# A sparse expert stage on one Trainium2 core: even down products right behind the pair's sum, and expert 0's rows turned inside the second gather

## The chip, the core and the metric

The kernel runs on one core of a Trainium2 chip. The metric is the device time in microseconds of one execution. In the profile PE is TensorE, DVE VectorE, ACT ScalarE, POOL GpSimd and SP the sync engine, whose queue (SPq) issues nearly all loads.

## What is computed

Two layers of a diffusion transformer on 256 tokens of width 1024 in float32: layer 0 has differential attention over tokens and context, layer 1 a pooling mixer, and behind each stands a mixture of 32 experts of which every token uses two. The reference, cut to the expert part:

```python
def moe(h_flat, router_w, router_b, w_gate, w_up, w_down):
    experts, gates = route(h_flat, router_w, router_b)      # 2 of 32 for each of 256 tokens
    ...                                                     # rows sorted by expert
    def expert_block(args):
        xb, e = args
        return (jax.nn.silu(xb @ w_gate[e]) * (xb @ w_up[e])) @ w_down[e]
    ys = lax.map(expert_block, (xs, block_e)).reshape(n_slots, d)
    ys = ys * slot_gate[:, None].astype(ys.dtype)
    return jax.ops.segment_sum(ys, slot_tok, num_segments=n + 1)[:n]
```

The weights w_gate and w_up are 1024 x 512 each and w_down is 512 x 1024, so an expert is 6 MB and a layer's experts are 201 MB.

## The kernel before

It is written out by engine, with semaphores; each engine follows its own list, and the order of that list is the schedule. The expert stage (`experts(L)` in each engine's part, run once per layer) goes so:

**Rows.** The 512 token-expert rows, sorted by expert, are gathered into `dense` by products of the tokens with 0/1 selections, in two halves of 256 rows, eight column blocks each (`gather_high`, `gather_low`; `spread` on ScalarE and `spread_v` on VectorE write the blocks out of PSUM with the modulation, odd and even blocks). Each expert is given 64 rows; GpSimd copies its window out of `dense` into one of two buffers `xw`, and counts `xw_ready`. Expert 0 is read from `dense` directly.

**One expert** on TensorE: the gate/up product in two halves of four blocks (`gate_up`, L825, 16 instructions a half, counted by `gu_half` and `gu_done`); ScalarE's silu (L1205) and VectorE's product (`hidden`, L1773) give the hidden rows `h_sb` (`h_ready`); TensorE turns them (`transposes`, L835, `tr_done`); ScalarE copies them from PSUM to `t_sb` (L1199, for the first expert L1191, `t_ready`); then the down product (`down`, L844, `dn_done`); VectorE multiplies it by the output gate (`gated_outputs`, L1755, `y_v`).

**Pairs.** Experts 2n and 2n+1 put their outputs side by side in `y_sb`, 64 rows each, and one product with the turned selection of 128 rows adds both to four PSUM banks (`combine`, L853, 8 instructions, half f = 0, then half f = 1). The selection `sg` of a pair is made on VectorE (`choose`, L1740 and L1744), turned on TensorE (L833, ahead of the hidden rows in the same PSUM bank) and copied with them; the copy is then 512 wide and not 256. In this kernel it is turned with the even expert of the pair.

**The order on TensorE**, in `step(e, c, it)`: transposes of expert e, first gate/up half of e+1, down of e, second gate/up half of e+1, and for odd e the whole sum. A loop of `TURNS` = 5 turns runs six such steps, experts 1 to 30, and a last step follows for expert 31. Expert 0 comes before: first gate/up, the second gather, its transposes with the selection, down, gate/up of expert 1.

**Weights** lie in three slots; expert e uses slot (e + layer) mod 3. The sync queue (`load_expert`, L325 and L330) issues for each expert the first halves of gate and up (2 x 1 MB) once `gu_half` says that expert e-3 is through with them, the second halves by `gu_done`, and the down weights (2 MB) by `dn_done`, strictly in that order. Three experts are loaded before a stage begins. Behind layer 0's experts the queue issues the weights of the pool stage (L405, L406, L409) and a table `inv_n` (L428).

## Time and profile before

| | us |
|---|---|
| timed runs: median of 3 | 1314.6 |
| lowest and highest | 1310.32, 1315.19 |
| profiled execution | 1308.68 |
| its span, first to last instruction | 1306.9 |
| TensorE matmul busy | 1200.5 (92%) |
| VectorE, ScalarE, GpSimd busy | 458.7, 178.4, 73.4 |
| moved by DMA | 485.5 MB, mean 371 GB/s |
| mean granted TensorE clock | 0.982 |

The expert stages lie at about 296 to 757 us (layer 0) and 841 to 1304 us (layer 1) of the span. Times in rows count from the span's start. The profile models the end of a matmul, so neighbouring rows of TensorE overlap a little; differences of starts are the safer measure. A bracket at the end of a row gives the idle time of the engine ahead of it and who ended it.

### The profile page before, as it was taken

The page shows a single profiled execution, that of the slowest core. Times are in us where ns is not written, and L with a number is a line of the kernel's source. Part 1 is how long each engine was busy: PE and PEld are TensorE (multiplying, and loading weights), DVE is VectorE, ACT ScalarE, POOL GpSimd, SP SyncE. Part 2 cuts the span into 40 slices and gives each one's busy share as a digit, 9 for nine tenths or more (in the row PEclk, how much of TensorE's full clock was granted, in tenths as well). Part 3 has the DMA queues.
Part 4 walks back from the last instruction along what each step waited for, and adds up shares of the span by engine and source line. Part 5 has one row for each costly group of instructions (what it writes and reads, how often), then busy time and mean ns, then how long its engine had stood idle before and what let it go on. Part 6 is the DMA issues. An engine that isn't in the chain of part 4 may idle for free.

```text
span 1306.9 us, 13664 instructions
## 1 busy us (share of the span) xinstructions
PE 1200.5 (92%) x5008; PEld 492.8 (38%) x5008; DVE 458.7 (35%) x933; ACT 178.4 (14%) x375; POOL 73.4 (6%) x86
## 2 busy tenths in 40 slices
PE   6999999889999999898998899899999998988897
PEld 3444445544333333232332376443333332322232
DVE  4296676577122212121121156642222221211112
ACT  2212126522000000000000021310000000000000
POOL 0113100000000000000000000000000000000000
PEclk9999999999999999899998999999999998999999
DMA  9948759286999999999999997589999999999995
GB/s 355 399 184 347 261 205 401 97 346 251 410 422 421 422 423 422 421 422 422 422 422 423 418 406 297 222 329 415 422 422 422 422 421 422 422 422 422 422 422 235
DMA packets 80933, 485.50 MB, mean 371 GB/s; under 512 B 6146, under 2 KB 7682, under 8 KB 31748
## 3 DMA queue, kind: packets, MB, share of 16 engines
q1 hardware_dynamic: 79168, 481.91, 90.3%
q10 hardware_dynamic: 1732, 3.16, 0.7%
q8 instruction: 20, 0.33, 0.1%
q14 instruction: 13, 0.11, 0.0%
HBM read 484.00 MB, written 1.05 MB: 371 GB/s over the span
## 4 chain that ended last, share of the span: by engine, by line
PE 57%; SPq 18%; DMA 15%; DVE 4%; issue 3%; ACT 3%; POOL 0%; DVEq 0%; ACTq 0%
PE PS L825 19%; SPq L325 14%; DMA ring<-in_moe_w_up 13%; PE PS L844 10%; PE PS L635 8%; PE PS L853 4%; SPq L330 3%; PE PS L605 2%; PE PS L707 2%; PE PS L997 2%; PE PS L972 2%; DMA ring<-in_attn_w_in 2%; PE PS L835 1%; DVE KQH L1773 1%; ACT ring L1071 1%
## 5 line engine op out<-in xcount | busy, mean ns | idle before, releaser
L825 PE MATMUL PS<-ring,KQH 128*64 128x512 f32 x2048 | 480.5, 613 | 30.1 <-DMA ring<-in_moe_w_up 28.6
L825 PEld LDWEIGHTS PS<-ring,KQH 128*64 128x64 f32 x2048 | 146.1, 141 | 311.0 <-issue 277.0
L844 PE MATMUL PS<-ring,KQH 128*64 128x512 f32 x1024 | 230.8, 592 | 2.3 <-ACT KQH L1191 1.4
L844 PEld LDWEIGHTS PS<-ring,KQH 128*64 128x64 f32 x1024 | 73.0, 137 | 147.8 <-issue 144.6
L1755 DVE TENSOR_TENSOR TMP<-PS,KQH 64x512 f32<-64x512 f32 x64 | 44.1, 689 | 228.8 <-PE PS L844 227.8
L1755 DVE TENSOR_TENSOR TMP<-PS,TMP 64x512 f32<-64x512 f32 x64 | 44.1, 689 | 227.8 <-PE PS L844 226.7
L853 PE MATMUL PS<-TMP,KQH 128*128 128x512 f32 x256 | 118.4, 605 | 1.6 <-DVE TMP L1755 1.6
L1205 ACT ACTIVATE KQH<-PS 128x256 f32<-128x256 f32 x62 | 23.8, 384 | 665.5 <-PE PS L825 646.0
L635 PE MATMUL PS<-ring,KQH 128*128 128x512 f32 x256 | 114.0, 593 | 0.0
L1773 DVE TENSOR_TENSOR KQH<-KQH,PS 128x256 f32<-128x256 f32 x64 | 38.7, 605 | 157.3 <-ACT KQH L1205 157.3
L465 POOL COPY KQH<-KQH 128x512 f32 x62 | 38.1, 617 | 831.5 <-PE PS L825 771.2
L853 PEld LDWEIGHTS PS<-TMP,KQH 128*128 128x128 f32 x256 | 46.0, 189 | 73.6 <-issue 70.3
L635 PEld LDWEIGHTS PS<-ring,KQH 128*128 128x128 f32 x256 | 46.5, 190 | 54.0 <-issue 54.0
L1740 DVE TENSOR_SCALAR rope_g<-const,route 128x128 f32<-128x128 f32 x128 | 35.7, 342 | 76.1 <-PE PS L835 75.7
L835 PE MATMUL PS<-const,KQH 128*128 128x128 f32 x128 | 26.2, 287 | 34.0 <-DVE KQH L1773 34.0
L448 POOL TENSOR_TENSOR stat<-stat,mhalf 128x16 f32<-128x16 f32 (+3 forms) x18 | 35.0, 1942 | 361.3 <-DVE stat L1546 130.8
L1366 DVE SCALAR_TENSOR_TENSOR ring<-ring,ccols 128x1024 f32<-128x1024 f32 x42 | 54.0, 1285 | 3.3 <-DMA ring<-in_ada_w 1.8
L1199 ACT COPY KQH<-PS 128x256 f32<-128x256 f32 (+1 forms) x62 | 29.5, 476 | 147.4 <-PE PS L835 147.4
L835 PEld LDWEIGHTS PS<-const,KQH 128*128 128x128 f32 x128 | 14.4, 140 | 61.4 <-DVE KQH L1773 61.4
L605 PE MATMUL PS<-ring,KQH 128*128 128x512 f32 x64 | 29.4, 619 | 1.8 <-DMA ring<-in_attn_w_in 1.8
L707 PE MATMUL PS<-ring,KQH 128*128 128x512 f32 x64 | 28.0, 594 | 0.9 <-ACT KQH L1078 0.9
L972 PE MATMUL PS<-KQH,ring 128*128 128x257 f32 x128 | 28.2, 379 | 0.0
(249 smaller groups left out, 788.0 us busy)
## 6 DMA issues: line engine op xcount, KB each, us to landing
ring<-in_moe_w_gate SPq DMA_DIRECT2D x128, 1024.0 KB, 26.5
ring<-in_moe_w_up SPq DMA_DIRECT2D x128, 1024.0 KB, 26.6
ring<-in_moe_w_down SPq DMA_DIRECT2D x64, 2048.0 KB, 27.9
ring<-in_ada_w SPq DMA_DIRECT2D x23, 2048.0 KB, 13.3
ring<-in_attn_w_in SPq DMA_DIRECT2D x2, 4096.0 KB, 12.7
ring<-in_attn_w_in SPq DMA_DIRECT2D x2, 2048.0 KB, 21.0
ring<-in_attn_w_out SPq DMA_DIRECT2D x1, 4096.0 KB, 24.1
ring<-in_pool_w_in SPq DMA_DIRECT2D x1, 4096.0 KB, 27.9
```

The source lines that it names most:

```text
L325: sp.dma_start(gu_w[s][:, a, 4 * part:4 * part + 4, :], w[L.l, e].rearrange("(p k) f -> p k f", p=P)[:, 4 * part:4 * part + 4, :]).then_in ...
L605: ins = mm(bank(4 + 2 * n + half), hT[:, k, P * n:P * n + P], unit(2)[:, k, 512 * half:512 * half + 512], start=k == 0, stop=k == KC - 1)
L635: ins = mm(bank(4 + 2 * (n % 2) + half), hT[:, k, P * t:P * t + P], unit(u)[:, k, 512 * half:512 * half + 512], start=k == 0, stop=k == KC ...
L707: ins = mm(bank(4 + q), oT[:, h, P * (q // 2):P * (q // 2) + P], unit(2)[:, h, 512 * (q % 2):512 * (q % 2) + 512], start=h == 0, stop=h == ...
L825: ins = mm(PS[64 * f:64 * f + 64, 4, :], xs[:, k, 0:SLOTS], gu_w[s][:, :, k, 256 * f:256 * f + 256], start=k == 0, stop=k == KC - 1)
L835: ins = tr(PS[:, 5, 256 + P * c:256 + P * c + P], h_sb[:, P * c:P * c + P], ident)
L844: ins = mm(PS[64 * f:64 * f + 64, 6, :], lhs, dn_w[s][:, c, 512 * f:512 * f + 512], start=c == 0, stop=c == 3)
L853: ins = mm(bank(2 * t + f), t_sb[:, P * t:P * t + P], y_sb[:, 512 * f:512 * f + 512], start=False, stop=done is not None, skip_group_check ...
L972: ins = mm(PS[:, n % 4, 0:SEQ + 1], pool_w[:, k, P * b:P * b + P], xa[:, k, :], start=k == 0, stop=k == KC - 1)
L1366: ins = V.scalar_tensor_tensor(acc, unit(u)[:, k, :], ccols[:, 32 * k:32 * k + 1], acc, ALU.mult, ALU.add)
L1755: return V.tensor_tensor(y_sb[64 * second:64 * second + 64, 512 * f:512 * f + 512], PS[64 * f:64 * f + 64, 6, :], g[64 * f:64 * f + 64, 51 ...
L1773: V.tensor_tensor(h_pairs, silu_sb.rearrange("p (q b) -> p q b", b=2), PS[:, 4, 256:512].rearrange("p (q b) -> p q b", b=2), ALU.mult).the ...
```

## The change

On TensorE the second gather is cut behind its fourth block: the hidden rows of expert 0 are turned there, without the selection, and blocks 4 to 7 follow. The selection of a pair is turned with the odd expert. The first pair has down products ahead of the gate/up that followed before. For each pair after it: transposes of the odd expert e (with the selection), first gate/up half of e+1, down of e, second half of e+1, the sum's half f = 0, transposes of e+1, the sum's half f = 1, down of e+1, and both gate/up halves of e+2. In the last two such pairs the odd down also goes ahead of the gate/up. The loop has one turn less, and its last pairs are written out. ScalarE's wide copy goes to the odd expert, VectorE's `choose` too, and VectorE begins its steps with a wait on `mod_used`, which it counts itself.

```diff
-            def combine(L, y, done=None):
-
-                for f in range(2):
-                    pe.wait_ge(L.y_v, y + f + 1)
-                    for t in range(NT):
...
+            def combine(L, y, f, done=None):
+
+                pe.wait_ge(L.y_v, y + f + 1)
+                for t in range(NT):
...
+            def second_places(L, k):
+
+                for t in range(NT):
+                    gather_high(1, k, t)
+                    ins = gather_low(1, k, t)
+                ins.then_inc(L.xg_done, 1)
+
+            def turn_hidden(L, e, c, it):
+
+                pe.wait_ge(L.h_ready, e + 1)
+                if c % 2:
+                    pe.wait_ge(L.sg_ready, 3 * it + (c // 2 + 1))
+                transposes(sg if c % 2 else None).then_inc(L.tr_done, 1)
+
+            def gate_up_first(L, e, c, it):
+
+                pe.wait_ge(L.gu_in[L.slot(c)], (2 * it + c // 3) * 32 + 32)
+                pe.wait_ge(L.xw_ready, e)
+                gate_up(L.slot(c), xw[c % 2], range(4)).then_inc(L.gu_half, 1)
+
+            def gate_up_second(L, e, c, it):
+
+                pe.wait_ge(L.gu2_in[L.slot(c)], (2 * it + c // 3) * 32 + 32)
+                gate_up(L.slot(c), xw[c % 2], range(4, KC)).then_inc(L.gu_done, 1)
+
+            def down_product(L, e, c, it):
+
+                pe.wait_ge(L.t_ready, e + 1)
+                pe.wait_ge(L.dn_in[L.slot(c)], (2 * it + c // 3) * 16 + 16)
+                pe.wait_ge(L.y_v, 2 * e)
+                down(L.slot(c)).then_inc(L.dn_done, 1)
+
+            def sum_and_next(L, e, c, it):
+
+                combine(L, 2 * e, 0)
+                turn_hidden(L, e + 1, c + 1, it)
+                combine(L, 2 * e, 1)
+                down_product(L, e + 1, c + 1, it)
+                gate_up_first(L, e + 2, c + 2, it)
+                gate_up_second(L, e + 2, c + 2, it)
...
-                for k in range(KC):
+                for k in range(4):
                     if k == 3:
                         pe.wait_ge(L.slots_known, 1)
...
+                    second_places(L, k)
                 pe.wait_ge(L.h_ready, 1)
-                pe.wait_ge(L.sg_ready, 1)
-                transposes(sg).then_inc(L.tr_done, 1)
+                transposes(None).then_inc(L.tr_done, 1)
+                for k in range(4, KC):
+                    pe.wait_ge((L.xs_v, L.xs_a)[k % 2], k // 2 + 3)
+                    second_places(L, k)
                 pe.wait_ge(L.t_ready, 1)
                 pe.wait_ge(L.xs_v, 7)
                 pe.wait_ge(L.dn_in[L.slot(0)], 16)
                 down(L.slot(0)).then_inc(L.dn_done, 1)
...
+                turn_hidden(L, 1, 1, 0)
+                down_product(L, 1, 1, 0)
+                gate_up_first(L, 2, 2, 0)
+                gate_up_second(L, 2, 2, 0)
+                sum_and_next(L, 1, 1, 0)
+
+                def pair(e, c, it, down_first=False):
+
+                    turn_hidden(L, e, c, it)
+                    if down_first:
+                        down_product(L, e, c, it)
+                    gate_up_first(L, e + 1, c + 1, it)
+                    if not down_first:
+                        down_product(L, e, c, it)
+                    gate_up_second(L, e + 1, c + 1, it)
+                    sum_and_next(L, e, c, it)
+
+                with pe.Fori(0, TURNS - 1) as it:
+                    for c in range(3, BODY + 3, 2):
+                        pair(BODY * it + c, c, it)
+                for c in (3, 5):
+                    pair(BODY * (TURNS - 1) + c, c, TURNS - 1, down_first=True)
+                turn_hidden(L, NE - 1, 1, TURNS)
+                down_product(L, NE - 1, 1, TURNS)
+                for f in range(2):
+                    combine(L, 2 * NE - 2, f, L.acc_done)
...
-                nc.scalar.copy(t_sb, PS[:, 5, :]).then_inc(L.t_ready, 1)
+                nc.scalar.copy(t_sb[:, 256:512], PS[:, 5, 256:512]).then_inc(L.t_ready, 1)
...
-                        a = 256 * (c % 2)
+                        a = 256 * (1 - c % 2)
...
+                dve.wait_ge(mod_used, TURN[LATE[L.l]] + 1)
 
                 def step(e, c, it, last=False):
-                    if c % 2 == 0 and not isinstance(it, int):
+                    if c % 2 and not last:
...
+                step(0, 0, 0)
                 with dve.Fori(0, TURNS) as it:
-                    for c in range(BODY):
+                    for c in range(1, BODY + 1):
                         step(BODY * it + c, c, it)
-                step(BODY * TURNS, 0, TURNS)
                 step(BODY * TURNS + 1, 1, TURNS, last=True)
```

## Rows read from the trace of the kernel before

**Rows 1.** The page: chain of waits by engine; GB/s in 40 slices of 32.7 us.
```profile
PE 57%; SPq 18%; DMA 15%; DVE 4%; issue 3%; ACT 3%; POOL 0%; DVEq 0%; ACTq 0%
...
GB/s 355 399 184 347 261 205 401 97 346 251 410 422 421 422 423 422 421 422 422 422 422 423 418 406 297 222 329 415 422 422 422 422 421 422 422 422 422 422 422 235
```

**Rows 2.** Timeline of TensorE, layer 0: start us, us, engine, line, operation, count, idle before.
```profile
380.09 3.65 PE L825 MATMUL PS<-ring,KQH 128*64 128x512 f32 x16
...
390.54 3.70 PE L853 MATMUL PS<-TMP,KQH 128*128 128x512 f32 x8
...
401.52 3.60 PE L825 MATMUL PS<-ring,KQH 128*64 128x512 f32 x16
406.25 0.44 PE L835 MATMUL PS<-const,KQH 128*128 128x128 f32 x2 [1.12 <-DVE KQH L1773]
406.62 3.65 PE L825 MATMUL PS<-ring,KQH 128*64 128x512 f32 x16
```

**Rows 3.** The same timeline, layer 1, late: first gate/up halves that waited for weights.
```profile
1207.69 3.65 PE L825 MATMUL PS<-ring,KQH 128*64 128x512 f32 x16 [1.55 <-DMA ring<-in_moe_w_up]
...
1237.51 6.50 PE L825 MATMUL PS<-ring,KQH 128*64 128x512 f32 x16 [2.85 <-DMA ring<-in_moe_w_up]
...
1267.33 3.65 PE L825 MATMUL PS<-ring,KQH 128*64 128x512 f32 x16 [0.38 <-DMA ring<-in_moe_w_up]
```

**Rows 4.** Timelines of TensorE, VectorE and GpSimd at the start of layer 0's stage.
```profile
313.92 0.38 PE L835 MATMUL PS<-const,KQH 128*128 128x128 f32 x2
314.97 3.65 PE L844 MATMUL PS<-ring,KQH 128*64 128x512 f32 x16 [0.68 <-ACT KQH L1191]
318.46 7.04 PE L825 MATMUL PS<-ring,KQH 128*64 128x512 f32 x32
...
326.66 0.44 PE L835 MATMUL PS<-const,KQH 128*128 128x128 f32 x2 [0.20 <-DVE KQH L1773]
...
311.08 0.62 DVE L1773 TENSOR_TENSOR KQH<-KQH,PS 128x256 f32<-128x256 f32 x1
...
316.34 1.17 POOL L465 COPY KQH<-KQH 128x512 f32 x2 [30.14 <-DVE KQH L1782]
```

**Rows 5.** Windows: stretch, length, PE busy (instructions), PE clock, DMA share, GB/s.
```profile
317.00:322.00 5.00, 5.00 (x26) 1.00 0.68 228
334.00:338.00 4.00, 4.00 (x19) 1.00 0.97 322
...
863.00:867.00 4.00, 4.00 (x22) 1.00 0.64 190
879.00:884.00 5.00, 5.00 (x21) 1.00 0.90 313
```

**Rows 6.** Timeline of the sync queue: issues of the down weights of experts 3 and 4.
```profile
318.67 0.38 SPq L330 DMA_DIRECT2D ring<-in_moe_w_down  x1
...
334.16 0.38 SPq L330 DMA_DIRECT2D ring<-in_moe_w_down  x1
```

**Rows 7.** Timeline of TensorE, end of layer 1: expert 31's gate/up halves and down product.
```profile
1282.24 3.65 PE L825 MATMUL PS<-ring,KQH 128*64 128x512 f32 x16 [0.32 <-DMA ring<-in_moe_w_up]
...
1289.15 3.60 PE L825 MATMUL PS<-ring,KQH 128*64 128x512 f32 x16
...
1294.77 3.65 PE L844 MATMUL PS<-ring,KQH 128*64 128x512 f32 x16 [0.46 <-ACT KQH L1199]
```

**Rows 8.** Pool stage: issue line L406 with its landing; timelines of TensorE and VectorE.
```profile
L406 SPq DMA_DIRECT2D ring<-in_pool_w_group x1: 12232/12232/12232, 728.7 to 728.7; - x1
...
DMA to landing us min/median/max: 30.5/30.5/30.5
...
759.92 3.64 PE L972 MATMUL PS<-KQH,ring 128*128 128x257 f32 x16
...
771.32 0.43 DVE L1570 COPY KQH<-PS 128x256 f32<-128x256 f32 x1 [7.32 <-DMA TMP<-in_inv_n]
...
788.95 0.42 DVE L1571 TENSOR_TENSOR KQH<-PS,KQH 128x256 f32<-128x256 f32 x1 [1.18 <-PE PS L972]
```

More of the change, by code:

```diff
@@ L846, in down @@
                 return ins
-            def combine(L, y, done=None):
-                for f in range(2):
-                    pe.wait_ge(L.y_v, y + f + 1)
-                    for t in range(NT):
-                        ins = mm(bank(2 * t + f), t_sb[:, P * t:P * t + P], y_sb[:, 512 * f:512 * f + 512], start=False,
-                                 stop=done is not None, skip_group_check=True)
-                        if done is not None:
-                            ins.then_inc(done, 1)
+            def combine(L, y, f, done=None):
+                pe.wait_ge(L.y_v, y + f + 1)
+                for t in range(NT):
+                    ins = mm(bank(2 * t + f), t_sb[:, P * t:P * t + P], y_sb[:, 512 * f:512 * f + 512], start=False,
+                             stop=done is not None, skip_group_check=True)
+                    if done is not None:
+                        ins.then_inc(done, 1)
@@ L889, in experts @@
                 pe.wait_ge(L.picked, 4)
-                for k in range(KC):
+                for k in range(4):
                     if k == 3:
                         pe.wait_ge(L.slots_known, 1)
-                    if k >= 4:
-                        pe.wait_ge((L.xs_v, L.xs_a)[k % 2], 4 + (k - 4) // 2 + 1)
-                    for t in range(NT):
-                        gather_high(1, k, t)
-                        ins = gather_low(1, k, t)
-                    ins.then_inc(L.xg_done, 1)
+                    second_places(L, k)
                 pe.wait_ge(L.h_ready, 1)
-                pe.wait_ge(L.sg_ready, 1)
-                transposes(sg).then_inc(L.tr_done, 1)
+                transposes(None).then_inc(L.tr_done, 1)
+                for k in range(4, KC):
+                    pe.wait_ge((L.xs_v, L.xs_a)[k % 2], k // 2 + 3)
+                    second_places(L, k)
                 pe.wait_ge(L.t_ready, 1)
@@ L905, in experts @@
                 down(L.slot(0)).then_inc(L.dn_done, 1)
-                pe.wait_ge(L.gu_in[L.slot(1)], 32)
-                pe.wait_ge(L.xw_ready, 1)
-                gate_up(L.slot(1), xw[1], range(4)).then_inc(L.gu_half, 1)
-                pe.wait_ge(L.gu2_in[L.slot(1)], 32)
-                gate_up(L.slot(1), xw[1], range(4, KC)).then_inc(L.gu_done, 1)
+                gate_up_first(L, 1, 1, 0)
+                gate_up_second(L, 1, 1, 0)
                 pe.wait_ge(L.xs_a, 8)
@@ L913, in experts @@
                 add_zero(False)
-                def step(e, c, it, last=False):
-                    n = c + 1
-                    pe.wait_ge(L.h_ready, e + 1)
-                    if c % 2 == 0:
-                        pe.wait_ge(L.sg_ready, 3 * it + (c // 2 + 1))
-                    transposes(None if c % 2 else sg).then_inc(L.tr_done, 1)
-                    if not last:
-                        pe.wait_ge(L.gu_in[L.slot(n)], (2 * it + n // 3) * 32 + 32)
-                        pe.wait_ge(L.xw_ready, e + 1)
-                        gate_up(L.slot(n), xw[n % 2], range(4)).then_inc(L.gu_half, 1)
-                    pe.wait_ge(L.t_ready, e + 1)
-                    pe.wait_ge(L.dn_in[L.slot(c)], (2 * it + c // 3) * 16 + 16)
-                    if c % 2:
-                        pe.wait_ge(L.y_v, 2 * e)
-                    down(L.slot(c)).then_inc(L.dn_done, 1)
-                    if not last:
-                        pe.wait_ge(L.gu2_in[L.slot(n)], (2 * it + n // 3) * 32 + 32)
-                        gate_up(L.slot(n), xw[n % 2], range(4, KC)).then_inc(L.gu_done, 1)
-                    if c % 2:
-                        combine(L, 2 * e, L.acc_done if last else None)
@@ L937, in experts @@
-                with pe.Fori(0, TURNS) as it:
-                    for c in range(1, BODY + 1):
-                        step(BODY * it + c, c, it)
-                step(BODY * TURNS + 1, 1, TURNS, last=True)
+                turn_hidden(L, 1, 1, 0)
[12 more added lines that the diff above has]
+                    sum_and_next(L, e, c, it)
```

## The prediction

> **What bounds the kernel now.** I read the page's chain of waits and its line of transfer rates first. The chain is split between TensorE (57%) and two names that mean the same thing, the sync queue issuing expert weights and those weights landing (18% and 15%), and the rate stands at 422 GB/s in nearly every slice of both expert stages [rows 1]. So two limits lie close together, and the question is which of them ends last where the change acts. The timeline of TensorE early in a stage gives its own pace: from the gate/up product at 380.09 to the one two experts later at 406.62 is 26.53 us a pair, with one idle gap of 1.12 us (the transposes that wait for the hidden rows of VectorE) and no wait for a transfer [rows 2]. Late in the stage TensorE does wait for transfers, and two first halves of gate/up begin 14.91 us apart (1267.33 and 1282.24), so 29.8 us a pair [rows 3, 7]. An expert is three loads of 2 MB (half the gate and up weights, the other half, the down weights), so each lands 14.91/3 = 4.97 us after the one before.
>
> TensorE is thus 3.3 us a pair faster than the weights. It starts each stage on three experts loaded beforehand, uses them up over half the stage, and from then on walks behind the loads. From the start of a stage the transfers run at their limit but for the gaps that the windows show: 5 us at 228 GB/s and 4 us at 322 in layer 0, 4 us at 190 and 5 us at 313 in layer 1 [rows 5]. Against 422 those are 2.30, 0.95, 2.20 and 1.29 us of lost transfer time. Everything that shortens such a gap brings every later load forward by as much; everything that only makes TensorE faster in the middle brings nothing. The other place where time can be won is behind the last loads, where TensorE works alone.
>
> **Start of a stage: the second gather.** Now TensorE gathers eight column blocks, turns expert 0's selection and hidden rows (four transposes), waits 0.68 us for ScalarE to copy them and begins expert 0's down product at 314.97 [rows 4]. The change takes two of the four transposes away (the selection is turned later, with expert 1) and puts the other two behind the fourth block. The hidden rows are ready at 311.08 + 0.62 = 311.70 [rows 4]; four of eight blocks end close to that time, so I count no wait. The copy, 256 wide, then hides under blocks 4 to 7. The down product starts where the second pair of transposes starts now, 313.92: 1.05 us earlier, of which I keep 1.0. VectorE's and ScalarE's last spreads move by the 0.2 us of the two transposes. That matters at one place: the first window copies of GpSimd wait for them, begin at 316.34 now and take 1.17 us for two [rows 4]; moved to about 317.8 at their end they stand close to the gate/up of expert 1, which would now begin at 318.46 - 1.0 = 317.4. Its own window, the first of the two, is ready near 317.2. Cover is 0.2 us; without it up to 0.4 us of TensorE's gain would go, but not of the transfer's, which hangs on the down product.
>
> The sync queue issues expert 3's down weights when expert 0's down product is done: at 318.67 [rows 6], in the middle of the first gap [rows 5]. They go out 1.0 us earlier, so 1.0 us of that gap closes in each layer.
>
> **Start of a stage: down before gate/up for expert 1.** Now expert 1's turn is transposes at 326.66, gate/up half, down, and the down weights of expert 4 are issued at 334.16 [rows 4, 6], at the second gap. The new order puts the down product right behind the transposes. It exposes the copy (0.68 us as above, the same four transposes) and then runs 3.4 us: 326.66 - 1.0 + 0.4 + 0.7 + 3.5 = 330.3. The issue comes 3.9 us earlier, more than the gap and the wait behind it together, so the gap closes: 0.95 us in layer 0, 1.29 in layer 1. The gate/up halves that follow finish one down product (3.4 us) later than in the old order, and expert 5's first loads with them; but the old queue stood behind the down weights until 334.16 anyway [rows 6]. New time 330.3 + 3.5 = 333.8, no loss. Bounds for what the start gives: nothing (if both gaps are refilled by another wait) and both gaps whole, 3.25 and 3.49 us. I take 1.95 and 2.29, nearest to the rows of the two gaps.
>
> **Middle of a stage.** Per pair the counts stay: four gate/up halves, two downs, four sums, six transposes, two copies. The sum is cut in two with the even transposes between its halves; hidden rows are ready 4.72 us after the last gate/up half starts (406.25 - 401.52 [rows 2]), the first half of the sum (3.70 us whole) ends 3.5 + 1.8 = 5.3 us after that start, so nothing is waited for; the second half, 1.8 us, covers the 0.4 us copy. On VectorE the choice of a selection moves from the even to the odd turn, ahead of its wait for the down product, and runs under a gate/up half. The pair stays at 26.5 us, and even if it cost 1 us more the loads at 29.8 would hide it. What changes is where TensorE is idle: the 3.3 us of slack, now in two places, fall together ahead of the gate/up that follows an odd expert's transposes. Row 1237.51 has the price of such a wait: after 2.85 us (and 1.12 before it) the half took 6.50 us instead of 3.65, at the lower granted clock; after 1.55 us it did not [rows 3]. Paid every pair this is 26.53 + 2.85 = 29.4 us, still under 29.8. Cost taken: nothing.
>
> The Trainium skill (TensorE: Matmul & The Clock Gate, HAM oscillation) speaks against such a layout: it says that one long wait for weights per group of matmuls brings the array back to half rate each time, and to keep work dense instead. The trace agrees in kind at 1237.51. By the rule every late pair would begin at half rate; by the sum just made the loads still end last, so it changes a rival below and not the forecast.
>
> **End of a stage.** The last pairs also have odd downs ahead of the gate/up. Call T the time when the first half of expert 31's gate/up weights is there, 1282.24 [rows 7]. Now: first half at T, expert 30's down, second half, hidden rows, copy, and expert 31's down at 1294.77, T + 12.53. New: expert 30's down is ahead of T. Counted from the landing for expert 30, T - 14.91: first half, second half at +4.97, half a sum at +8.5, transposes at +10.3, half a sum at +10.5, down at +12.3, free at +15.7, so T + 0.8. First half until T + 4.3; the second half must wait for its weights until T + 4.97; from there to the down product it is what it is now, 4.72 + 0.90 = 5.62 (1289.15 to 1294.77 [rows 7]). Down at T + 10.59, its weights being there at T + 9.94. Gain 1.94 us. Bounds: 0 if expert 30's or 31's first half runs at the lower clock and the second half waits for it rather than for weights, 2.6 if the landing alone decided.
>
> **Behind layer 0.** Stage 0 would end 1.95 + 1.94 = 3.89 us earlier, but the pool stage waits for transfers that only move with the loads, by 1.95 us. The last of its group weights land at 728.7 + 30.5 = 759.2, and TensorE begins with them at 759.92, 0.7 us later [rows 8]: some of the 3.89 must be given back there. VectorE begins its pool sums at 771.32, after waiting 7.32 us for a table queued behind the pool weights, and has 1.18 us of slack at the last block [rows 8]. So at most 1.95 + 1.18 = 3.13 us come through. The rest of layer 0 and the routing of layer 1 move with that.
>
> **Sum.** 3.13 (layer 0) + 2.29 + 1.94 (layer 1) = 7.36 us. The profiled execution took 1308.68 us (span 1306.9); it would be 1301.3. The median of the three timed runs, 1314.6, is 5.9 us above it, and the runs go from 1310.32 to 1315.19; none of my terms depends on that difference, so the median becomes 1307.2.
>
> **Rivals.**
> Only the start pays. The last products run at the lower clock, or the last down weights come later than I count. For: the new order holds idle time together, and one slowed half (2.85 us) takes more than the 1.94. Against: in the last pairs the odd down splits the wait (some 1.1 us ahead of expert 30's half by the count above), and 1.55 us was harmless [rows 3]. Layers 0 and 1 give 1.95 + 2.29 = 4.2: 1310.4.
>
> Nothing to speak of. The gaps are filled by the next wait in line, since gate/up of the even expert now comes after the down and the queue takes waits in order. For: 422 GB/s is held through most of each stage whatever TensorE does [rows 1], so moves of 3 us are invisible there. Against: the gaps are real in the rows. Gain under 2.5: about 1313.
>
> More than forecast. Both gaps close whole, which adds 1.2 us in layer 1 and about as much of layer 0 as its pool stage lets through: 9 us, 1305.6.
>
> Slower. The clock falls not only where TensorE waits for weights but in each pair, because transposes and half sums now break up the dense stretch. It decides from 3.3 us a pair on, that is if more than the first half (2.85) runs at the lower rate: with two halves, 5.7 us, a pair is 32.2 us, 2.4 over the loads, in some 15 pairs a layer: +70 us. Only in the last three pairs of each layer, the least that would show, it is 2 x 3 x 2.4 = 14.4 us less the 4.2 us of the starts: 1324.8, the time I give this rival. Against: the present order has the same 1.12 us gap and a full clock wherever no weights are awaited [rows 2], and a late TensorE does not idle, so the state heals itself.
>
> **How the numbers follow.** Forecast as reckoned 50%, start only 23%, nothing 11%, more 10%, slower 6%. About 0.5% (6.6 us) is what a measurement of this kernel can tell from no change, and the forecast lies close to it: of its 50 points I give 40 to faster by over 0.5% and 10 to within; more gives 10 to faster; start only and nothing give 34 to within. Faster 50, same 44, slower 6. Range: below, the profiled execution's own level with 9 us gained, 1299.7; above, the median with 1 us gained, 1313.6.
>
> **What would show it.** Right: expert 3's down weights issued 1.0 us, expert 4's 3.9 us closer to the stage's first product; windows there at about 1.3 us and 0 us of lost transfer; 26.5 us a pair before the weights are used up, and after that one wait of about 3 us a pair, often with a half of 6.5 us behind it; 10.6 us from expert 31's first half being landed to its down product; VectorE's wait of 1.18 us at the last pool block gone. Wrong: gaps of the old length behind earlier issues, a pair above 26.8 us at full clock, or a window copy that holds expert 1 by more than 0.5 us.

## The result and the profile after

The changed kernel takes 1302.9 us (median; 1302.34 to 1303.26), the kernel before 1313.2 us in the same rounds (1310.32 to 1315.19). The ratio is 0.9925, 95% interval 0.991 to 0.994: faster by 0.75%, 10.3 us. The forecast was 1307.2 us, range 1299.7 to 1313.6. So the sign and the range held and the gain, forecast at 7.4 us, was larger. Of the 4.3 us between 1307.2 and 1302.9, 1.4 is the level: the forecast was taken off 1314.6, the median of three runs, and this measurement has 1313.2. The other 2.9 are gain. But the two profiled executions are only 6.1 us apart (1308.68 and 1302.56): less than forecast. That contradiction is the subject of most of what follows.

The page of the kernel after, with total busy times, the line of transfer rates, the head of the chain of waits, and the groups of the expert stage (line, engine, output<-input, count, busy time, mean ns of one, idle time ahead of them and what ended it):

```profile
span 1300.8 us, 13648 instructions
PE 1196.2 (92%) x5006; PEld 488.9 (38%) x5008; DVE 459.4 (35%) x933; ACT 178.4 (14%) x375; POOL 73.2 (6%) x86
...
GB/s 352 402 182 348 264 201 401 111 328 262 423 422 421 421 422 421 422 422 421 422 422 421 418 406 308 240 335 422 420 422 421 422 422 422 421 422 422 422 421 252
...
PE 53%; SPq 30%; DMA 8%; DVE 3%; ACT 3%; issue 2%; POOL 0%; DVEq 0%; ACTq 0%
...
L825 PE MATMUL PS<-ring,KQH 128*64 128x512 f32 x2048 | 468.0, 605 | 23.6 <-DMA ring<-in_moe_w_up 22.0
...
L844 PE MATMUL PS<-ring,KQH 128*64 128x512 f32 x1024 | 232.6, 596 | 5.4 <-ACT KQH L1233 5.4
```

The stage still stands between two limits: 422 GB/s in nearly every slice, now in the slice at the start of layer 0's experts too (423, where [rows 1] has 410), and a TensorE that waits 22.0 us in all for gate/up weights. New is the wait of 5.4 us for ScalarE's copy, 8 times 0.67 us, at the places where a down product follows its transposes at once.

The start of layer 0's stage, timeline of TensorE (the turn of expert 0; the down product of expert 0, gate/up of expert 1, the down products of experts 1 and 2), and the sync queue's issues of the down weights of experts 3, 4 and 5:

```profile
311.73 0.41 PE L835 MATMUL PS<-const,KQH 128*128 128x128 f32 x2
...
313.97 3.65 PE L844 MATMUL PS<-ring,KQH 128*64 128x512 f32 x16
317.45 7.04 PE L825 MATMUL PS<-ring,KQH 128*64 128x512 f32 x32
...
327.00 3.65 PE L844 MATMUL PS<-ring,KQH 128*64 128x512 f32 x16 [0.67 <-ACT KQH L1233]
...
341.30 3.65 PE L844 MATMUL PS<-ring,KQH 128*64 128x512 f32 x16
```
```profile
317.66 0.38 SPq L330 DMA_DIRECT2D ring<-in_moe_w_down  x1
...
330.69 0.38 SPq L330 DMA_DIRECT2D ring<-in_moe_w_down  x1
...
345.00 0.38 SPq L330 DMA_DIRECT2D ring<-in_moe_w_down  x1
```

The turn in the middle of the gather waits for nothing, and the down product follows the last block at once: 1.00 us earlier than in [rows 4]. The down weights of expert 3 are issued 1.0 us earlier than in [rows 6], those of expert 4 3.5 us earlier (330.69 against 334.16). The windows that answer to [rows 5] (last number: GB/s; layer 1's stage now begins 2.5 us earlier, so its windows are moved):

```profile
317.00:322.00 5.00, 5.00 (x26) 1.75 (x24) 1.98 (x3) 0.00 (x0) 0.69 (x2) 1.00 0.88 308
334.00:338.00 4.00, 4.00 (x20) 1.24 (x17) 0.02 (x1) 0.38 (x1) 0.00 (x0) 1.00 1.02 422
862.00:866.00 4.00, 4.00 (x22) 1.38 (x20) 0.00 (x0) 0.00 (x0) 0.00 (x0) 1.00 0.92 358
876.00:882.00 6.00, 6.00 (x24) 1.97 (x21) 0.61 (x1) 0.38 (x1) 0.61 (x1) 1.00 1.01 421
```

The second gap is gone in both layers. Of the first, ten microseconds from 314 on now run at 371 GB/s (before 328), and in layer 1 at 369 (331): 1.0 and 0.9 us won. A check over a longer stretch, the forty microseconds that begin 4 us behind the stage's first gate/up: 392 GB/s in both layers, where before has 373 and 369, so 1.8 and 2.2 us won in all.

The end of layer 0's experts, timeline of TensorE. 719.37 and 724.34 are the gate/up halves of expert 30, 739.24 is the second half of expert 31, 745.34 its down product:

```profile
719.37 3.65 PE L825 MATMUL PS<-ring,KQH 128*64 128x512 f32 x16 [0.18 <-DMA ring<-in_moe_w_up]
724.34 3.65 PE L825 MATMUL PS<-ring,KQH 128*64 128x512 f32 x16 [1.31 <-DMA ring<-in_moe_w_up]
...
739.24 3.65 PE L825 MATMUL PS<-ring,KQH 128*64 128x512 f32 x16 [0.38 <-DMA ring<-in_moe_w_up]
744.01 0.44 PE L833 MATMUL PS<-const,KQH 128*128 128x128 f32 x2 [1.12 <-DVE KQH L1807]
744.28 0.38 PE L835 MATMUL PS<-const,KQH 128*128 128x128 f32 x2
745.34 3.65 PE L844 MATMUL PS<-ring,KQH 128*64 128x512 f32 x16 [0.68 <-ACT KQH L1233]
```

The second half now waits for its weights, as forecast, so the last landing sets the end. Behind it stands what the forecast missed: the selection is turned here too (L833, two more transposes) and copied (0.68 us for 512 columns, where [rows 7] has 0.46 for 256). From the second half to the down product it is 6.10 us, not 5.62.

### The profile page after: what moved, and what is told of

Same layout as the page of the kernel before. It is cut to its first block, busy times and chain, and to the rows that moved or that the text cites. A ratio compares the mean times of both kernels' runs of the same rounds, so it can differ in the third digit from the quotient of the medians.

```text
span 1300.8 us, 13648 instructions
## 1 busy us (share of the span) xinstructions
PE 1196.2 (92%) x5006; PEld 488.9 (38%) x5008; DVE 459.4 (35%) x933; ACT 178.4 (14%) x375; POOL 73.2 (6%) x86
## 3 DMA queue, kind: packets, MB, share of 16 engines
q10 hardware_dynamic: 1732, 3.16, 0.7%
## 4 chain that ended last, share of the span: by engine, by line
PE 53%; SPq 30%; DMA 8%; DVE 3%; ACT 3%; issue 2%; POOL 0%; DVEq 0%; ACTq 0%
SPq L325 24%; PE PS L825 17%; PE PS L635 8%; PE PS L844 8%; SPq L330 5%; DMA ring<-in_moe_w_up 4%; PE PS L852 4%; DMA ring<-in_pool_w_group 3%; PE PS L605 2%; PE PS L1006 2%; PE PS L707 2%; PE PS L1031 2%; DMA ring<-in_attn_w_in 2%; DVE KQH L1807 1%; PE PS L814 1%
## 5 line engine op out<-in xcount | busy, mean ns | idle before, releaser
L825 PE MATMUL PS<-ring,KQH 128*64 128x512 f32 x2048 | 468.0, 605 | 23.6 <-DMA ring<-in_moe_w_up 22.0
L844 PE MATMUL PS<-ring,KQH 128*64 128x512 f32 x1024 | 232.6, 596 | 5.4 <-ACT KQH L1233 5.4
L852 PE MATMUL PS<-TMP,KQH 128*128 128x512 f32 x256 | 123.4, 606 | 1.6 <-DVE TMP L1789 1.6
L833 PE MATMUL PS<-const,KQH 128*128 128x128 f32 x64 | 13.9, 299 | 35.8 <-DVE KQH L1807 35.8
L1233 ACT COPY KQH<-PS 128x512 f32<-128x512 f32 (+1 forms) x62 | 29.9, 482 | 98.2 <-PE PS L835 98.2
L833 PEld LDWEIGHTS PS<-const,KQH 128*128 128x128 f32 x64 | 6.5, 140 | 63.1 <-issue 49.7
```

Of the source, the lines that this page charges most:

```text
L825: ins = mm(PS[64 * f:64 * f + 64, 4, :], xs[:, k, 0:SLOTS], gu_w[s][:, :, k, 256 * f:256 * f + 256], start=k == 0, stop=k == KC - 1)
L844: ins = mm(PS[64 * f:64 * f + 64, 6, :], lhs, dn_w[s][:, c, 512 * f:512 * f + 512], start=c == 0, stop=c == 3)
L852: ins = mm(bank(2 * t + f), t_sb[:, P * t:P * t + P], y_sb[:, 512 * f:512 * f + 512], start=False, stop=done is not None, skip_group_check ...
```

## The experiments

All intervals below are differences of starts in one profile: from a stage's first gate/up product to expert 31's down product. The table gathers them, with the median of each kernel. The ratios are to runs of before in the same set, and the sets differ a little: the median of before is 1312.4 us beside again, oldtail, filler and notail, 1312.1 beside after2, nostart, startonly and ends, and 1311.5 beside ends2, earlysg and again2. Again2 and nostart2 are single executions, taken for their profiles.

| run | median us (lowest, highest) | ratio, 95% interval | layer 0 | layer 1 |
|---|---|---|---|---|
| before | 1313.2 | | 445.75 | 446.76 |
| again | 1311.8 (1310.4, 1314.4) | 0.9998, 0.9986 to 1.0009 | 446.76 | 448.51 |
| again2 | one run, 1312.4 | | 449.12 | 446.74 |
| startonly | 1310.5 (1307.1, 1312.3) | 0.9986, 0.9976 to 0.9996 | 446.36 | 448.51 |
| oldtail | 1309.9 (1305.7, 1310.9) | 0.9981, 0.9971 to 0.9991 | 444.42 | 444.84 |
| ends | 1306.2 (1302.6, 1307.7) | 0.9948, 0.9927 to 0.997 | 443.99 | 444.54 |
| ends2 | 1302.7 (1302.5, 1304.5) | 0.9929, 0.9906 to 0.9952 | 443.87 | 442.72 |
| filler | 1311.2 (1308.9, 1312.3) | 0.9986, 0.9973 to 1.0 | 447.25 | 446.82 |
| after | 1302.9 (1302.3, 1303.3) | 0.9925, 0.991 to 0.994 | 442.64 | 443.21 |
| after2 | 1301.8 (1301.5, 1303.7) | 0.9928, 0.9911 to 0.9944 | 442.71 | 442.85 |
| notail | 1306.0 (1304.1, 1307.6) | 0.995, 0.9935 to 0.9966 | 446.08 | 443.98 |
| nostart | 1308.2 (1306.6, 1309.5) | 0.9969, 0.9957 to 0.9981 | 444.92 | 444.11 |
| nostart2 | one run, 1308.2 | | 445.91 | 444.50 |
| earlysg | 1302.1 (1300.1, 1303.1) | 0.9923, 0.9902 to 0.9944 | 442.29 | 442.65 |

**The kernel before, unchanged, again** (again, again2).

> The kernel before, once more and unchanged, to see where its executions differ: they went from 1308.68 to 1315.19 us, those of the changed kernel only from 1302.34 to 1303.26. Ratio 1.00. Theory of the clock: the differences arise where TensorE waits about 2.8 us for weights ahead of expert 30's first gate/up half; in some executions that half takes up to 6.5 us and not 3.65, expert 31's first half then starts up to 2.5 us after its weights are there, and the layer ends that much later, so up to 5 us for two layers. Its profile then shows one of two things at the end of a layer: a 3.65 us half with expert 31's half waiting 0.3 us for weights (fast), or a slowed half and expert 31's half waiting for nothing (slow). Rival: the spread comes from elsewhere (attention, transfers at less than 422 GB/s), and both ends of layers look as in the first profile whatever the time.

> The kernel before once more, for its layer ends. Theory (near the last experts the old order sometimes runs a half of gate/up at the lower clock, and then finishes a layer 1 to 2 us later): a half of 5 us or more within the last three experts in at least one layer, and expert 31's down product there 446.5 us or more after the stage's first gate/up; where no half is slow, 445.8 to 446.8. Rival (the end of a layer hangs on the landing alone): the same interval in both layers whatever the halves take.

The executions of before go from 1308.46 to 1316.65 us over 59 timed runs in three sets; one of the 59 is below the 1308.68 of the profile on which the forecast was made. Its layers took 445.75 and 446.76 us; in again and again2 they took up to 449.12. What differs is the half of gate/up of expert 30. TensorE in again2, layer 0 (722.11 is that half, 739.55 the first half of expert 31, 752.09 the last down product):

```profile
722.11 6.58 PE L825 MATMUL PS<-ring,KQH 128*64 128x512 f32 x16 [2.84 <-DMA ring<-in_moe_w_up]
...
739.55 3.65 PE L825 MATMUL PS<-ring,KQH 128*64 128x512 f32 x16
...
752.09 3.65 PE L844 MATMUL PS<-ring,KQH 128*64 128x512 f32 x16 [0.46 <-ACT KQH L1199]
```

After a wait of 2.84 us the half takes 6.58 us, and expert 31's half then has no wait: the weights were there and TensorE came late. A slowed half in the middle of a stage only uses up the next wait; one in the last pair is paid but for the 0.3 us that expert 31's half would have waited. So the landing alone does not set the end in the old order. In the six layers profiled, expert 30's half was slowed in three: 446.76, 448.51 and 449.12 us; in the other three it was not: 445.75, 446.76 and 446.74. The two groups touch, since the weights themselves land up to 1.0 us apart from layer to layer (expert 30's half begins between 418.29 and 419.32 us of the stage). Counted from there, 14.91 us on, expert 31's half began 1.0, 2.5 and 2.5 us late in the three slowed layers: an estimate of 2.0 us a profile.

Which half is slowed goes by turns. In the first profile of before it was expert 28's in both layers, and the lateness that it left made the wait ahead of expert 30 short (layer 0; layer 1 is in [rows 3]):

```profile
691.25 6.56 PE L825 MATMUL PS<-ring,KQH 128*64 128x512 f32 x16 [2.84 <-DMA ring<-in_moe_w_up]
...
721.06 3.65 PE L825 MATMUL PS<-ring,KQH 128*64 128x512 f32 x16 [0.30 <-DMA ring<-in_moe_w_up]
```

In the ten layers that end in the old order without added products (before, again, again2, startonly, notail) expert 30's half was slowed in the six where expert 28's was not, and in none of the four where it was. In the sixteen layers with the down products of the last pairs first (oldtail, ends, ends2, after, after2, nostart, nostart2, earlysg) no half of experts 30 and 31 was slowed. The four of after and after2 lie within 0.57 us of each other.

**The start alone, both ends, and the third gap** (startonly, ends, ends2). To the kernel before are added the turn inside the gather (with the selection) and down products ahead of the gate/up (`down_first`): of expert 1 in startonly, of experts 1, 29 and 30 in ends, and of expert 2 as well in ends2. The middle keeps the old order.

```diff
+                    if k == 4:
+                        pe.wait_ge(L.h_ready, 1)
+                        pe.wait_ge(L.sg_ready, 1)
+                        transposes(sg).then_inc(L.tr_done, 1)
...
+                step(1, 1, 0, down_first=True)
+                step(2, 2, 0)                           # ends2: down_first=True here too
...
+                for c in range(3, BODY + 1):            # ends and ends2
+                    step(BODY * (TURNS - 1) + c, c, TURNS - 1, down_first=c >= 5)
```

> The kernel before with the start alone: the second gather cut behind block 4 with all four transposes of expert 0 there, and expert 1's down product ahead of the gate/up. Middle and end as before. Theory: expert 3's down weights issued 0.8 us earlier, expert 4's 3.9; the gaps at 1.5 and 0 us; layer 0 gives 1.75, layer 1 2.1: 3.8 us off the 1312.4 of the kernel before, 1308.6, with its wide spread. Rival (only the ends pay): 1312.4.

> The kernel before with start and end but with its own middle: the selection is turned with the even expert, the sum stays whole, expert 1 and experts 29 and 30 have their down product first. Theory (the middle is hidden under the weights, only start and ends count): as fast as the changed kernel or a little faster, since expert 31 is turned without the selection: 5.6 us from its second half being landed to its down product for 6.1, and 0.2 us lost at expert 0 for the two more transposes in the gather: 1302.5. Rival (the new middle carries gain of its own): 1305 or more.

> Starts and tails as in the run ends, plus one thing more: expert 2's down product ahead of the gate/up of expert 3. Theory (a third gap opens where expert 5's down weights wait for expert 2's down product, and only the new order of the first pairs closes it): the ten microseconds behind the second gap, 401 GB/s in ends, come back to 421 or 422 in both layers; expert 31's down product 443.2 to 443.7 us after the stage's first gate/up instead of 444.0 and 444.5; median about 2 us under ends, 1304. Rival (the third gap is the queue's own, whatever the order of the products): that window stays near 401 GB/s and the median at 1306. What is then left between this kernel and the changed one is the middle order alone: 1 us or less if the middle gives nothing.

Startonly brought 1.6 us against its set's median of 1312.1, less than half of what the two gaps promise (4.2), and ends stood at 1306.2 where 1302.5 was expected. The rates tell where the better part of it went. Windows behind the second gap, of startonly, ends and ends2, in this order (last number: GB/s):

```profile
339.00:359.00 20.00, 18.88 (x87) 6.61 (x87) 3.52 (x8) 1.34 (x3) 0.62 (x1) 1.00 1.00 403
885.00:905.00 20.00, 18.88 (x87) 6.62 (x87) 3.52 (x8) 1.34 (x3) 0.61 (x1) 1.00 0.99 399
```
```profile
340.00:360.00 20.00, 18.88 (x85) 6.54 (x86) 3.52 (x8) 1.34 (x3) 0.62 (x1) 1.00 0.99 401
884.00:904.00 20.00, 18.88 (x87) 6.57 (x87) 3.52 (x8) 1.34 (x3) 0.61 (x1) 1.00 0.99 404
```
```profile
340.00:360.00 20.00, 18.20 (x85) 6.32 (x85) 3.52 (x8) 1.34 (x3) 0.61 (x1) 1.00 1.01 422
884.00:904.00 20.00, 18.21 (x85) 6.13 (x85) 3.52 (x8) 1.34 (x3) 0.61 (x1) 1.00 1.01 423
```

At 401 instead of 422 GB/s, twenty microseconds lose 1.0 us. With the first two gaps closed, a third opens: the down weights of expert 5 wait for expert 2's down product, which in the old order comes behind half a gate/up of expert 3. One step's order (ends2 against ends) closes it in both layers, and the median falls from 1306.2 to 1302.7 us (in sets whose medians of before are 1312.1 and 1311.5), to that of the changed kernel. Of that 2 us are the gap. In layer 1 the interval falls by 1.8, in layer 0 by only 0.1, where a half slowed to 5.35 us came late (690.09). Ends2 has the old order in all middle pairs, and a ratio to before of 0.9929 against 0.9925 and 0.9928 for the changed kernel: the new middle order is worth nothing that can be measured.

**The tail alone** (oldtail: the kernel before with experts 29 and 30 down first; notail: the changed kernel without that).

```diff
- pair(BODY * (TURNS - 1) + c, c, TURNS - 1, down_first=True)
+ pair(BODY * (TURNS - 1) + c, c, TURNS - 1)                    # notail
```

> The kernel before with one thing done: the steps of experts 29 and 30 have their down product ahead of the gate/up (written out behind a loop of four turns); start and middle as before. Theory of the ends: from expert 31's second half being landed to its down product 5.6 us, and that half 1.9 us earlier than in the kernel before; layer 0 keeps only the 1.2 us of slack of its pool stage, layer 1 all 1.9: 3.1 us off the profiled 1308.7, so 1305.6 for an execution like that one. With the theory of the clock the median falls by more, from 1313.2 to about 1307, and the spread to 1 or 2 us. Rival (only the start pays): 1313, no change.

> The changed kernel with one part undone: its last two pairs are ordinary ones, with the odd down product between the gate/up halves. Theory of the ends: down of expert 29 now sits behind expert 30's first half, so down of expert 30 ends 2.7 us after expert 31's first weights land and not 0.8; its second half then starts at +6.2 us, not +5.0: 1.2 us a layer, 1305.2. With the clock theory the long wait is ahead of expert 30's half again and costs up to 2.85 us more a layer in some executions: 1305 to 1310 and a spread of several us. Rival (only the start pays): 1302.9, no change.

Oldtail against the profile of before, which had no slowed half of experts 30 and 31: 1.33 and 1.92 us a layer, at the forecast's 1.94 or below it. Notail against after: 3.44 in layer 0 and 0.77 in layer 1. Of the 3.44, 2.0 stand in one row, expert 30's half in notail; from its start to expert 30's down product it is 16.33 us, in layer 1 14.31:

```profile
720.75 5.68 PE L825 MATMUL PS<-ring,KQH 128*64 128x512 f32 x16 [3.38 <-DMA ring<-in_moe_w_up]
```

Layer 1's had [1.53] and 3.65 us. So the tail's order gives two things: a down product out of the way, and a split of the long wait (0.18 and 1.31 in the rows of after above, where notail has 3.38). Only the first was in the sum. By the medians the tail is worth 3.9 us (notail lies 6.4 us under its set's before, the changed kernel 10.3). Oldtail's profile took 1305.69 us, where 1305.6 was expected, but it is the lowest of its ten executions. The theory of the clock expected a median near 1307 and a spread of 1 to 2 us; the median was 1309.9 and the spread 5.3. That part of the theory failed, and I can't tell why.

**The start undone** (nostart, nostart2: the changed kernel with the gather uncut and expert 1's down product behind the first half again).

```diff
-                for k in range(4):
+                for k in range(KC):
...
                 turn_hidden(L, 1, 1, 0)
-                down_product(L, 1, 1, 0)
                 gate_up_first(L, 2, 2, 0)
+                down_product(L, 1, 1, 0)
                 gate_up_second(L, 2, 2, 0)
```

> The changed kernel with the start undone: expert 0's hidden rows turned behind all eight gather blocks, and expert 1's down product between the gate/up halves of expert 2. The selection is still turned later, so expert 0's down product comes 0.5 us after that of the changed kernel and not 1.0. Theory of the gaps: lost transfer time in the first gap 1.7 us for 1.2 to 1.35, the second gap back at 0.9 to 1.3 us, all of it passed on: 1.4 us in layer 0, 1.8 in layer 1, 1306.1. Rival (transfers are refilled anyway, only the ends pay): 1302.9.

> The run nostart once more, for its last products. Its median lies 6.4 us above the changed kernel's, while the two start gaps, by their windows, account for 3.6. Theory (the rest is the clock at a layer's end): in at least one layer the last down product, or a half of expert 30 or 31, runs at the lower clock again, over 5 us instead of 3.65. Rival (that one slowed down product was chance, and the rest is something else): all products of the last two experts at 3.65 us in both layers, expert 31's down product 444.1 to 444.9 us after the stage's first gate/up, and the whole near 1306.

The median rises by 6.4 us against after2 in the same set; 3.2 were expected against 1302.9. By the rates 3.6 of that are transfer: ten microseconds at 346 instead of 371 and ten at 370 instead of 421 in layer 0, 342 instead of 369 and 374 instead of 422 in layer 1, together 151 GB/s x 10 us / 422 GB/s = 3.6 us. A part of the rest stands at the end of a layer. Nostart, layer 0, and nostart2, layer 1, the last down product in each:

```profile
747.33 5.35 PE L844 MATMUL PS<-ring,KQH 128*64 128x512 f32 x16 [0.68 <-ACT KQH L1233]
```
```profile
1291.22 0.44 PE L833 MATMUL PS<-const,KQH 128*128 128x128 f32 x2 [1.12 <-DVE KQH L1807]
...
1292.55 5.35 PE L844 MATMUL PS<-ring,KQH 128*64 128x512 f32 x16 [0.68 <-ACT KQH L1233]
```

1.7 us more than 3.65, in two of four layer ends, behind the intervals of the table, which end where it starts. In layer 0 of nostart2 the interval is 3.2 us above that of after2; its last weights landed 3.2 us later, of which the rates at the start explain 1.8. Profile against profile (1304.8 and 1306.4 against 1300.8 and 1299.6 us of span) the mean difference is 5.4 us: 4.0 in the two intervals, and most of the rest the slowed last product that each of the two has once. So about 1 us of the 6.4 is not accounted for. The four layers of after and after2, and the two of earlysg, have none of this in their last two experts. The theory's sign, a last product at the lower clock, came again, but the runs show a coincidence and not what causes it: why a start that is 2 us later brings the clock down at the end isn't shown.

**Keeping TensorE busy instead** (filler: the kernel before with three products whose result nobody reads, six instructions and 2.74 us in the profile, between the transposes and the gate/up half in the last three odd turns).

```diff
                     transposes(None if c % 2 else sg).then_inc(L.tr_done, 1)
+                    if filler:
+                        stay_busy(filler, 7)
```

> The kernel before with the last six steps of the loop written out and, in those of experts 25, 27 and 29, three products of constants (2.6 us, result unused) behind the transposes, where TensorE now waits for weights. The order of the work is untouched. Theory of the clock: the first halves of experts 26, 28 and 30 stay at 3.65 us, expert 31's half is never late, and all executions look like the fastest of the kernel before: median 1309 to 1310, spread 1 to 2 us, against 1313.2 and 6. Rival: the spread has nothing to do with it, median 1313 or, if the added products delay the down products, 1314 to 1316.

No half of the last experts was slowed, in either layer; expert 30's waits for 0.54 us after the added products and takes 3.65. But the first half of expert 31 begins at 434.71 us of the stage, 1.5 us later than in before (433.21), waiting for its weights; so the loads came later, and the interval is 447.25 us. The median fell by 1.2 us, at the edge of what was measured. The expected 1309 to 1310 us and the spread of 1 to 2 did not come: 1311.2 us and 3.4. The run agrees with the clock as a cost, since no half was slowed, and says little of its size.

**The changed kernel again, and the selection turned early** (after2, earlysg). Earlysg turns and copies the last pair's selection before the hidden rows are ready:

```diff
-                turn_hidden(L, NE - 1, 1, TURNS)
+                pe.wait_ge(L.sg_ready, 3 * TURNS + 1)
+                for t in range(NT):
+                    ins = tr(PS[:, 5, P * t:P * t + P], sg[:, t, :], ident)
+                ins.then_inc(L.sg_turned, 1)        # ScalarE copies it and counts on
+                pe.wait_ge(L.h_ready, NE)
+                pe.wait_ge(L.sg_turned, 2)
+                transposes(None).then_inc(L.tr_done, 1)
```

> The changed kernel again, unchanged, beside the others of this group. 1302.9 us, and a spread well below that of the kernel before (5 to 7 us): by the theory of the clock no slowed half can fall just ahead of the last products of a layer, so what is left is what comes from the attention stage, up to 2 us. Rival: its small spread (0.9 us in four executions) was luck, and it is as wide as the other.

> The changed kernel, but in the last turn of each layer the selection is turned and copied before the hidden rows are ready, so that behind them only two transposes and a copy 256 wide stand. Theory (the selection in the odd turn costs 0.48 us a layer at the tail): from the second half of expert 31's gate/up to its down product 5.6 us instead of 6.1 in both layers, median 0.5 to 1.0 us under the changed kernel's (about 1301.5). Rival (the wait of ScalarE's first copy, or the lower clock of a TensorE that idles longer, takes it back): 6.0 us or more and no difference in the median.

TensorE at the end of layer 0 in earlysg, second half of expert 31 to its down product:

```profile
739.23 3.65 PE L826 MATMUL PS<-ring,KQH 128*64 128x512 f32 x16 [0.36 <-DMA ring<-in_moe_w_up]
742.81 0.44 PE L974 MATMUL PS<-const,KQH 128*128 128x128 f32 x2
744.00 0.44 PE L836 MATMUL PS<-const,KQH 128*128 128x128 f32 x2 [0.75 <-DVE KQH L1817]
744.89 3.65 PE L845 MATMUL PS<-ring,KQH 128*64 128x512 f32 x16 [0.46 <-ACT KQH L1243]
```

5.66 us instead of 6.10, in layer 1 5.67: the missed term, 0.44 us a layer, is real and can be taken back. The median, 1302.1, lies between those of after2 and after (1301.8 and 1302.9), so a gain of 0.9 us at most doesn't show in it.

## Why the prediction was right in sign and short in size

**The first gap: right.** 1.0 us was forecast for each layer, 1.0 and 0.9 came. The window copy that I feared would hold expert 1 didn't: its gate/up follows the down product at 317.45 without a wait, where 317.4 was forecast.

**The second gap: right in size, with its condition unnamed.** 0.95 and 1.29 us were forecast; by ten-microsecond windows from 329 and 876 us on 1.0 and 1.35 came (381 and 365 GB/s, now 421 and 422). The issue came 3.5 us earlier, not 3.9: the transposes began at 325.67 as reckoned, but four of them take more than the 0.4 us that I put in (the down product began at 327.00, not 326.8), and the queue issues 0.2 us behind the product's end. What I didn't see is the third gap. I wrote that all that makes TensorE faster in the middle brings nothing. From the second pair on that held (ends2). For expert 2 it didn't: startonly and ends lose 1.0 us a layer at 401 GB/s. The forecast for the whole change was spared because the change moves that product too.

**The middle: right.** A pair takes 26.60 us (starts at 380.21 and 406.81), against 26.53 in [rows 2]. The long waits fell together as forecast, one of 3.16 us and a half of 6.44 behind it (629.91), and as forecast they cost nothing there. The Trainium skill's warning (TensorE: Matmul & The Clock Gate, HAM oscillation) is borne out in kind, but a slowed half eats most of the next pair's slack, so not every pair has one: in layer 0 they stand at 570.26 and 629.91 us in after and at 569.85, 599.65 and 659.25 in after2, and the pairs between, behind waits of 1.46 and 1.42 us, have 3.65.

**The end: the mechanism right, one term missed.** Forecast were T + 10.59 instead of T + 12.53. The second half did wait for its weights, but from there to the down product it was 6.10 us and not 5.62: I had counted the move of the selection to the odd turn in the middle, where it is hidden, and not in the last turn, where it isn't. The second half's weights of expert 31 came forward by 1.65 and 2.1 us (in before they are reckoned, T + 4.97) instead of 1.95 and 2.29. Both together are the difference of the intervals: 3.1 and 3.55 us gained, forecast 3.9 and 4.2.

**Behind layer 0: right.** From expert 31's down product to the next stage's first gate/up it takes 99.51 us before and 100.13 after: 0.6 us given back, forecast 0.8 (after2: 99.83, 0.3 given back). VectorE's wait of 1.18 us [rows 8] is not gone but 0.32, and its wait for the table has grown from 7.32 to 8.73:

```profile
769.57 0.42 DVE L1604 COPY KQH<-PS 128x256 f32<-128x256 f32 x1 [8.73 <-DMA TMP<-in_inv_n]
...
786.34 0.42 DVE L1605 TENSOR_TENSOR KQH<-PS,KQH 128x256 f32<-128x256 f32 x1 [0.32 <-PE PS L1006]
```

**The sum, profile against profile:** 3.1 - 0.6 + 3.55 = 6.1 us, forecast 7.36.

**From the profile to the median: wrong.** "None of my terms depends on that difference" is the step that failed. The profile of before was nearly the fastest execution there is, for a reason that the change acts on: no half of experts 30 and 31 was slowed in it, and in six of the ten layers with the old tail one was. Over the three profiles of before the intervals average 447.3 us, over those of after and after2 442.9: 4.4 us a layer, 8.8 in all, less 0.5 behind layer 0. Another 1.0 us is the start of layer 0's stage, on average 303.4 us before and 302.4 after; the change touches nothing ahead of it, and it goes from 302.1 to 304.6 in all the profiles. With 0.1 behind the last product that is 9.5 us, and the spans of these profiles differ on average by just that: 1309.7 and 1300.2. So of 9.5 us 6.1 are the steps that were forecast, as the first two profiles show them; 2.3 are layer ends of before that fell out worse than in its first profile (by the rows, a slowed half of expert 30 in three of four layers, whose lateness alone comes to 2.0 us a profile), and 1.1 is the scatter of the part ahead. The 2.3 is a difference of means over six and four layers and no firmer than that, and 0.8 of the 10.3 us between the medians stays open.

**The rivals.** "More than forecast" came nearest to the time (1305.6), for another reason than the one it named. "Only the start pays" is refuted by oldtail and notail, "nothing" (a gain under 2.5 us) by the 10.3 us and the rates, "slower" by the 26.60 us a pair.

## What to carry to other kernels

Where an engine walks behind its transfers, the middle is free and the two ends are not: each gap of the queue at the start counts in full, and closing one can open the next, so look at the windows behind it; and in the last turn no wait is left to absorb a slowed product or two transposes that were moved there. A profile is one execution: before its sum is carried to the median, ask which waits near the end fell out well in it, and whether the change takes the bad draws away: here they were some 2 of 9.5 us. That the changed kernel also scatters less (0.9 and 2.2 us in two sets of four runs, before 4.9 in four and 8.2 in 59) rests on few runs.

## What the runs showed of the hardware

**The lower clock behind waits of different length.** In the fourteen profiles of these kernels, every gate/up half behind a wait of 1.6 us or more for its weights took 5.0 us or more, 88 of 88; some 1.1 us of idle time and a pair or two of transposes come before such a wait, if it is a first half's. Behind waits of 1.30 to 1.57 us it was 3.65 in 43 of 47, and 5.35 in four (1.48, 1.53, 1.54 and 1.57 us). Windows of again2 around the half at 722.11 (third number from the end: granted clock):

```profile
716.00:722.00 6.00, 2.15 (x10) 0.49 (x6) 0.60 (x1) 0.76 (x2) 0.62 (x1) 0.93 1.01 422
722.00:725.00 3.00, 2.89 (x8) 1.00 (x10) 0.00 (x0) 0.00 (x0) 0.00 (x0) 0.50 1.01 418
725.00:729.00 4.00, 4.00 (x14) 1.04 (x12) 0.00 (x0) 0.00 (x0) 0.00 (x0) 0.62 1.02 424
729.00:733.00 4.00, 4.00 (x22) 1.36 (x20) 0.80 (x2) 0.00 (x0) 0.00 (x0) 1.00 1.01 422
```

TensorE had been busy for 2.15 of the 6 us before; the clock then stood at 0.50, 1.2 of 2.4 GHz, and was back at 1.00 by 729.

**The lower clock without a long wait.** I had not expected the last down product of nostart and nostart2 at 5.35 us: the idle times ahead of it are 0.39 (a wait for weights), 1.12 and 0.68 us. The same three idle times stand ahead of the last down product in both layers of after and after2, at 3.65. In layer 1 of nostart and of nostart2 expert 29's down product is slowed too (5.35 us at 1262.86 and 1262.24), behind 0.4, 1.12 and 0.68 us of idle time. That it is the clock shows in the windows of nostart2 around the product at 1292.55:

```profile
1290.00:1293.00 3.00, 1.21 (x8) 0.62 (x8) 0.60 (x1) 0.97 (x2) 0.00 (x0) 1.00 0.02 8
1293.00:1296.00 3.00, 3.00 (x10) 0.87 (x8) 0.00 (x0) 0.00 (x0) 0.00 (x0) 0.54 0.00 0
```

**Time and clock over executions.** Over the 28 executions of before that were timed beside again, time and mean granted clock go together with a correlation of -0.76: 1315.1 us on average at 0.979, 1311.0 at 0.984 (three runs each). In the sets of 19 and 12 it is -0.51 and -0.78. That is what slowed products would give, but which of them lay at the ends isn't known for executions without a profile.
